# Memory keys and values in another order, 512-column value matmuls, column norms, and three moved steps

## The reference

```
mkv  = rmsnorm(mem_prompt, g_mem) @ w_mem_kv          # 256 memory tokens -> 4 heads x 256 keys, 4 heads x 256 values
xn   = rmsnorm(x, g_mix);  cq, ... = split_in(xn @ w_in)
branch_c = softmax(cq . mk / 16) @ mv                 # prompt tokens against these keys and values
branch_b = attention of 8 query heads over the chosen keys   # softmax over key rows, two heads at a time
h    = x + merged @ w_out
u    = rmsnorm(h, g_ffn) @ w_up                       # then convolution, gate, w_down, final rmsnorm
```

## Time and profile before

| | us |
|---|---|
| median of three runs (2171.22 to 2172.59) | 2171.45 |
| the profiled execution | 2170.77 |
| its span on the core | 2169.2 |
| TensorE busy | 2152.0 (99%) |
| VectorE busy | 1222.6 (56%) |
| ScalarE busy | 904.4 (42%) |
| GpSimd busy | 103.9 (5%) |

### The profile page before, as it was taken

One profiled execution on the slowest core, in us unless ns is written; L12 is line 12 of the kernel. 1 busy time (PEld: TensorE's weight loads), 2 busy tenths in 40 slices (PEclk: granted clock), 3 DMA queues, 4 the chain that ended last, 5 costly groups with the idle time before them and its releaser, 6 DMA issues.

```text
span 2169.2 us, 40311 instructions
## 1 busy us (share of the span) xinstructions
PE 2152.0 (99%) x14759; PEld 2126.8 (98%) x14759; DVE 1222.6 (56%) x1928; ACT 904.4 (42%) x1520; POOL 103.9 (5%) x152
## 2 busy tenths in 40 slices
PE   9999999999999999999999999999999999999998
PEld 9999999999999999999999999999999999999998
DVE  8745655444644444444445666656665566656675
ACT  6434433333443333333333444444444444444455
POOL 2202300001300000000000000000000000000000
PEclk9999999999999999999999999999999999999999
DMA  8644444444334444444454444454444543454443
GB/s 292 222 160 129 159 149 135 146 136 135 103 127 155 146 156 148 145 155 147 154 195 146 138 143 155 137 170 138 154 126 157 163 148 131 152 166 144 150 138 126
DMA packets 96625, 329.43 MB, mean 152 GB/s; under 512 B 11656, under 2 KB 19976, under 8 KB 96400
## 3 DMA queue, kind: packets, MB, share of 16 engines
q1 hardware_dynamic: 92928, 315.97, 45.0%
q0 software_dynamic: 3456, 9.49, 1.5%
q10 hardware_dynamic: 144, 2.62, 0.3%
HBM read 321.30 MB, written 6.73 MB: 151 GB/s over the span
## 4 chain that ended last, share of the span: by engine, by line
PE 95%; DVE 3%; DMA 1%; ACT 1%; issue 0%; SPq 0%; DVEq 0%; ACTq 0%
PE bank L542 29%; PE bank L543 29%; PE bank L544 29%; PE bank L581 3%; PE bank L578 1%; DVE w_lo L1317 1%; PE bank L873 1%; PE bank L875 1%; PE bank L874 1%; PE bank L572 0%; DMA hT<-in_xT 0%; PE bank L573 0%; PE bank L574 0%; PE bank L561 0%; PE bank L562 0%; PE bank L563 0%
## 5 line engine op out<-in xcount | busy, mean ns | idle before, releaser
L542 PE MATMUL bank<-xn_hi,w_hi 128*128 128x320 f32 (+1 forms) x3088 | 958.6, 310 | 3.3 <-DVE w_lo L1317 3.3
L544 PE MATMUL bank<-xn_hi,w_lo 128*128 128x320 f32 (+1 forms) x3088 | 953.2, 309 | 0.0
L543 PE MATMUL bank<-xn_lo,w_hi 128*128 128x320 f32 (+1 forms) x3088 | 953.2, 309 | 0.0
L1317 DVE TENSOR_TENSOR w_lo<-w_raw,w_hi 128x1024 fp32r<-128x1024 f32 x625 | 745.1, 1229 | 344.3 <-ACT w_hi L924 342.4
L924 ACT CAST w_hi<-w_raw 128x1024 fp32r<-128x1024 f32 x625 | 631.2, 1047 | 177.4 <-PE bank L544 155.0
L542 PEld LDWEIGHTS bank<-xn_hi,w_hi 128*128 128x128 f32 x3088 | 580.5, 188 | 8.1 <-issue 3.1
L543 PEld LDWEIGHTS bank<-xn_lo,w_hi 128*128 128x128 f32 x3088 | 580.6, 188 | 0.4
L544 PEld LDWEIGHTS bank<-xn_hi,w_lo 128*128 128x128 f32 x3088 | 580.6, 188 | 0.0
L543 PE MATMUL bank<-y_lo,w_hi 128*128 128x320 f32 x616 | 189.9, 308 | 0.0
L544 PE MATMUL bank<-y_hi,w_lo 128*128 128x320 f32 x616 | 189.9, 308 | 0.0
L542 PE MATMUL bank<-y_hi,w_hi 128*128 128x320 f32 x616 | 189.9, 308 | 0.0
(11 more groups left out here) (329 smaller groups left out, 2085.7 us busy)
## 6 DMA issues: line engine op xcount, KB each, us to landing
w_raw<-in_w_in SPq DMA_DIRECT2D x210, 512.0 KB, 3.8
w_raw<-in_w_up SPq DMA_DIRECT2D x176, 512.0 KB, 3.7
w_raw<-in_w_down SPq DMA_DIRECT2D x64, 512.0 KB, 3.5
w_raw<-in_w_branch SPq DMA_DIRECT2D x48, 512.0 KB, 3.4
...
```

The lines of the kernel that those rows point to most:

```text
L542: pe.matmul(out, h, hi[:, k0 + k, c0:n], start=un == 0 and k == 0, stop=False)
L543: pe.matmul(out, h, lo[:, k0 + k, c0:n], start=False, stop=False)
L544: last = pe.matmul(out, l, hi[:, k0 + k, c0:n], start=False, stop=un == len(units) - 1 and k == nk - 1)
L1317: dve.tensor_tensor(wlo[:, pl.slot(j), :, :], raw[:, pl.slot(j), :, :], f32(whi[:, pl.slot(j), :, :]), ALU.subtract).then_inc(w_lo, 1)
```

## The change

- **Order of the memory units.** For each quarter of the memory rows come k of head 0, half of v of heads 0 and 1, k of head 1, and the other half; then k of head 2, eight units of v of heads 2 and 3, and k of head 3. A v unit now has 256 rows x 512 columns: 12 matmuls of 512 columns. Each token half has one of the banks G, and each head's keys have a bank of their own.
- **Norms.** TensorE sums the squares into columns (one value per partition, for 128 tokens at a time), DVE computes the inverse root on 2 or 3 columns, multiplies them into a diagonal, and TensorE spreads the diagonal over all partitions (`inverse_rows`, before units 14 and 21). The sums stand before units 12 and 19.
- **Steps around it.** The loads and splits of the memory tokens come two units later or so (SP 3, 5, 7 for 1, 3, 5), v is read out after units 16 and 28 (two heads at once), k after units 15, 16, 20 and 31, x is scaled after units 21 to 29, and the scores of branch C wait for all keys.
- **First query softmax.** `q_exps(0)` stands at tile 3, behind the casts of that tile.
- **hT.** The first two of its 16 row blocks come in a transfer of their own ahead of the rest.
- **sum(h^2).** The matmul stands between the two units of the first feed-forward tile instead of behind both.

```diff
-KV_UNITS = [(kind, 0, n) for n in range(4) for kind in "kv"] + [(kind, h, n) for h in range(1, CHD) for kind in "kv"
-                                                              for n in range(4)]
-KV_LAST = {j: (kind, h) for j, (kind, h, n) in enumerate(KV_UNITS) if n == 3}
-U_CQ, T_CQ = len(KV_UNITS), 2 * CHD
-MEM_SUM, X_SUM = 7, 19
+KV_UNITS = [u for n in range(4) for u in (("k", 0, n), ("v", 0, 2 * n), ("k", 1, n), ("v", 0, 2 * n + 1))]
+KV_UNITS += [("k", 2, n) for n in range(4)] + [("v", 1, n) for n in range(8)] + [("k", 3, n) for n in range(4)]
+KV_LAST = {(kind, h): j for j, (kind, h, n) in enumerate(KV_UNITS)}
+U_CQ, T_CQ = len(KV_UNITS), CHD
+MEM_SUM, MEM_ROW, X_SUM, X_ROW = 12, 14, 19, 21
...
-        nvar = sums_at("norm_var", [3, T])
+        nvar = sums_at("norm_var", [3, 4])
+        diag = sums_at("inverse_diagonal", [T])
...
+        K_BANKS = (M[4], M[5], M[2], M[3])
...
-            after = {1: (lambda: mem_chunk(1),), 3: (lambda: mem_chunk(2), identity), 5: (lambda: mem_chunk(3),),
+            after = {3: (lambda: mem_chunk(1),), 5: (lambda: mem_chunk(2), identity), 7: (lambda: mem_chunk(3),),
...
-            def k_unit(pl, t, j, un):
+            def k_unit(pl, head, j, un):
...
-                        out, c = G[pl.bank(t)][:, e * NMEM:e * NMEM + NMEM], slice(e * P, e * P + P)
+                        out, c = K_BANKS[head][:, e * NMEM:e * NMEM + NMEM], slice(e * P, e * P + P)
...
-            def v_unit(pl, t, j, un):
-                h, l = v_units(whi, pl.slot(j)), v_units(wlo, pl.slot(j))
-                for k in range(4):
+            def v_unit(pl, j, un):
+                h, l = (w[:, pl.slot(j), :, :].rearrange("p (k four) c -> p k (four c)", four=4) for w in (whi, wlo))
+                for k in range(2):
                     for m in range(2):
-                        out, tok = G[pl.bank(t)][:, m * 256:m * 256 + 256], slice(m * P, m * P + P)
-                        k_ = 4 * un + k
-                        pe.matmul(out, mhi[:, k_, tok], h[:, k, :], start=k_ == 0 and m == 0, stop=False)
+                        out, tok = G[m][:, :], slice(m * P, m * P + P)
+                        k_ = 2 * un + k
+                        pe.matmul(out, mhi[:, k_, tok], h[:, k, :], start=k_ == 0, stop=False)
                         pe.matmul(out, mhi[:, k_, tok], l[:, k, :], start=False, stop=False)
-                        last = pe.matmul(out, mlo[:, k_, tok], h[:, k, :], start=False, stop=k_ == KT - 1 and m == 1)
+                        last = pe.matmul(out, mlo[:, k_, tok], h[:, k, :], start=False, stop=k_ == KT - 1)
...
-            def square_sums(n, width):
+            def square_sums(n, starts):
                 pe.wait_ge(ident_in, 16)
                 pe.wait_ge(x_sum if n else t_sum, 1)
-                total, ones = sq_sum[:, n, 0:width], K[:, C_ONE:C_ONE + P]
-                last = mm(M[n][:, 0:width], ones, total)
-                if n == 0:
-                    for m in range(2):
-                        last = mm(M[0][:, NMEM + m:NMEM + m + 1], sq_sum[:, 0, m * P:m * P + P], ones[:, 0:1])
+                for u, t in enumerate(starts):
+                    last = mm(M[n][:, u:u + 1], sq_sum[:, n, t:t + P], K[:, C_ONE:C_ONE + 1])
                 last.then_inc(t_tot, 1)
+            def inverse_rows(n, width):
+                pe.wait_ge(t_dg, n + 1)
+                mm(M[n][:, 0:width], K[:, C_ONE:C_ONE + P], diag[:, 0:width]).then_inc(t_row, 1)
...
-                pe.wait_ge(c_kf, h + 1)
+                pe.wait_ge(c_kf, CHD)
...
                 if j == MEM_SUM:
-                    square_sums(0, NMEM)
+                    square_sums(0, (0, P))
+                if j == MEM_ROW:
+                    inverse_rows(0, NMEM)
                 if j == X_SUM:
-                    square_sums(1, T)
-                t = 2 * h + (kind == "v")
-                if un == 0:
-                    pe.wait_ge(bank_read[plc.bank(t)], plc.bank_free(t))
+                    square_sums(1, (0, P, T - P))
+                if j == X_ROW:
+                    inverse_rows(1, T)
+                if kind == "v" and un == 0:
+                    for m in range(2):
+                        pe.wait_ge(bank_read[m], plc.bank_free(2 * h + m))
                 pe.wait_ge(*((w_lo, plc.through(j)) if j else (lo_first, 1)))
-                (k_unit if kind == "k" else v_unit)(plc, t, j, un)
+                if kind == "k":
+                    k_unit(plc, h, j, un)
+                else:
+                    v_unit(plc, j, un)
...
-            multiply(pl, 0, [(0, xhi, xlo, 0, UK), (1, xhi, xlo, UK, UK)], T, parts=(h_lo, KT))
-            pe.wait_ge(h_sum, KT + 1)
-            mm(M[0][:, 0:T], K[:, C_ONE:C_ONE + P], hacc[:, 0:T]).then_inc(sums, 1)
+            def h_sums():
+                pe.wait_ge(h_sum, KT + 1)
+                mm(M[0][:, 0:T], K[:, C_ONE:C_ONE + P], hacc[:, 0:T]).then_inc(sums, 1)
+            multiply(pl, 0, [(0, xhi, xlo, 0, UK), (1, xhi, xlo, UK, UK)], T, parts=(h_lo, KT), between=h_sums)
...
+            def v_tokens(p):
+                act.wait_ge(t_inv, 1)
+                act.wait_ge(w_used, pl.through(KV_LAST["v", p]))
+                for m in range(2):
+                    act.activation(mv[:, 2 * p:2 * p + 2, m, :], G[m][:, :].rearrange("p (h c) -> p h c", h=2), ACT.Identity,
+                                   scale=mnv[:, m:m + 1]).then_inc(bank_read[m], 1)
+                for m in range(2):
+                    act.wait_ge(bank_read[m], pl.bank_read(2 * p + m))
+                act.sem_inc(c_mvn, 2)
+            after = {0: (lambda: mem_squares(0),), 1: (lambda: mem_chunk(1),), 2: (lambda: mem_squares(1),),
+                     4: (lambda: mem_chunk(2),), 6: (lambda: mem_squares(2),), 8: (lambda: mem_chunk(3),),
+                     9: (lambda: mem_squares(3),), 12: (lambda: root(1, 2, nvar),), 16: (lambda: v_tokens(0),),
+                     19: (lambda: root(2, 3, nvar),)}
+            for c in range(4):
+                after[10 + 2 * c] = after.get(10 + 2 * c, ()) + (lambda c=c: x_squares(c),)
+            for q in range(8):
+                after[21 + q] = after.get(21 + q, ()) + (lambda q=q: x_hi(q),)
+            after[KV_LAST["v", 1] + 1] += (lambda: v_tokens(1),)
...
+                if t == 3:
+                    q_exps(0)
...
-                    q_exps(i - 1)
+                    if t > 2:
+                        q_exps(i - 1)
...
-            act.dma_start(hT[:, :, :].rearrange("p k t -> p (k t)"), a["xT"]).then_inc(hT_in, 16)
+            for k0, k1, done in ((0, 2, hT_in), (2, KT, hT_rest)):
+                act.dma_start(hT[:, k0:k1, :].rearrange("p k t -> p (k t)"), a["xT"][:, k0 * T:k1 * T]).then_inc(done, 16)
...
-            def mem_inverse():
-                dve.wait_ge(t_tot, 1)
-                rms(0, NMEM + 2, M[0][:, 0:NMEM + 2], nvar)
+            def inverse_columns(n, widths):
+                cols = len(widths)
+                dve.wait_ge(t_tot, n + 1)
+                rms(n, cols, M[n][:, 0:cols], nvar)
                 own.settle()
-                dve.tensor_copy(mnv[:, :], nvar[:, 2, NMEM:NMEM + 2])
-                dve.tensor_copy(minv[:, :], nvar[:, 2, 0:NMEM]).then_inc(t_inv, 1)
-                dve.wait_ge(t_inv, 1)
-                dve.wait_ge(c_raw, 1)
-                dve.tensor_tensor(kf[:, 0, 0, :], kf[:, 0, 0, :], minv[:, :], ALU.mult)
-                dve.tensor_tensor(kf[:, 0, 1, :], kf[:, 0, 1, :], minv[:, :], ALU.mult).then_inc(c_kf, 1)
-            def x_inverse():
-                dve.wait_ge(t_tot, 2)
-                rms(1, T, M[1][:, 0:T], nvar)
+                if n == 0:
+                    dve.tensor_copy(mnv[:, :], nvar[:, 2, 0:2]).then_inc(t_inv, 1)
+                    dve.wait_ge(ident_in, 16)
+                else:
+                    dve.wait_ge(t_row, 1)
+                t = 0
+                for u, width in enumerate(widths):
+                    last = dve.tensor_scalar(diag[:, t:t + width], ident[:, P - width:P], nvar[:, 2, u:u + 1], None, ALU.mult)
+                    t += width
+                last.then_inc(t_dg, 1)
+            def inverse_row(n, out, width):
+                dve.wait_ge(t_row, n + 1)
+                own.did(dve.tensor_copy(out[:, :], M[n][:, 0:width]))
                 own.settle()
-                dve.tensor_copy(inv[:, :], nvar[:, 2, 0:T]).then_inc(t_inv, 1)
-                dve.wait_ge(t_inv, 2)
+            def k_features(h):
+                dve.wait_ge(w_used, pl.through(KV_LAST["k", h]))
+                for e in range(2):
+                    last = dve.tensor_tensor(kf[:, h, e, :], K_BANKS[h][:, e * NMEM:e * NMEM + NMEM], minv[:, :], ALU.mult)
+                last.then_inc(c_kf, 1)
...
-            after = {0: (lambda: square_part(0),), 1: (lambda: mem_los(4), lambda: mem_los(5)),
-                     2: (lambda: square_part(1),), 3: (lambda: mem_los(6), lambda: mem_los(7)),
-                     4: (lambda: square_part(2),), 5: (lambda: square_part(3), square_sum),
```

(19 more changed lines are left out.)

52 lines of the change are left out of this document (11 added, 41 removed).

## The result

| | before | after |
|---|---|---|
| median of the runs | 2171.22 us (5 runs, 2169.32 to 2172.59) | 2159.34 us (5 runs, 2159.13 to 2159.65) |
| ratio | | 0.9949, 95% interval 0.9938 to 0.9960 |
| profiled execution, its span | 2170.77 us, 2169.2 us | 2159.49 us, 2157.7 us |

A forecast was written before the change was run, and what follows sets the result against it. TensorE's matmul stream, busy 99% of the span, was taken as the bound; 2.5 + 3.8 + 1.6 + 1.0 + 3.7 - 0.75 = 11.85 us from 2170.77 gave 2158.9, stated as 2159.2, range 2155.8 to 2164.0.

The forecast's parts named there:

- Width: v units of the memory stage: 512-column matmuls at 226 ns remove 192 matmuls and save 2.5 us, bounds 0 to 5.0.
- The rival by the 2.5 ns of the Trainium skill: v matmuls: only 2.5 ns saved for each of 192, 0.5 us, giving 2161.2; width without gain had chance 0.12.
- Memory holes: Memory stage: three TensorE idle times of 1.19, 1.10 and 0.76 us, each plus 0.26, go; 3.8 us saved.
- the holes of 73.31 and 77.21: TensorE idle 1.10 and 0.76 us in the memory stage, blamed on DVE's 5.5 us norm of x ahead of `w_lo`.
- the first hole: TensorE idle 1.19 us at 39.75, memory stage: ACT waited 3.95 us for DVE's inverse rms before reading the first v.
- Small matmuls: Memory stage: six new single-column passes for x and two more returns to the stream cost 0.75 us, between 0.3 and 1.2.
- Softmax: Query stage: casts ahead of the first softmax remove TensorE's 1.35 us idle time plus 0.26; 1.6 us saved.
- hT: Output projection: a small first transfer ends DVE's 5.75 us wait for 2.6 MB; 0.75 + 0.26 = 1.0 us saved.
- Sum of h squared: Feed-forward start: the sum one unit earlier closes the 1.91 us hole and slow-clock stretch, with 0.5 us to spare; 3.7 us saved.
- The diagonal: Before memory units 14 and 21 TensorE waits for DVE's diagonal of inverse norms; claimed ready in time by 1 to 2 us.
- holes that came back: Memory-stage rival: late diagonal, late loads or DVE out of lead return up to 3.8 us; 2160 to 2163, chance 0.10.

## Why the prediction was right

**Width: right, a little too large.** Forecast 226 ns per 512 columns and 2.5 us; measured 228.2 ns and, with all else equal, 2.32 us. The rest beside the columns grew from 13 to 15 ns. The rival by the 2.5 ns of the Trainium skill, "TensorE: Matmul & The Clock Gate", section "Back-to-back issue gap" (an estimate of 512 / 2.4 + 2.5 = 215.8 ns per matmul), is refuted by this kernel's steps. The section gives that formula for a matmul by itself, which the prediction didn't say.

**Memory holes: right in size, half wrong in reason.** All three went. The 3.8 us were not measured for all three together; for the holes of 73.31 and 77.21, forecast at 2.4, the kernel with columns at the old place shows 94.87 - 92.89 + 0.41 = 2.4 us. But the step that gave these two holes to the narrow operations named one of two sufficient causes. The place alone does it, and the columns of x cost 0.41 us that the kernel needn't pay. Of the two cures the prediction counted on the dearer one. The reason given for the first hole, ACT's early read of v, was not undone by itself.

**Small matmuls: too large.** +0.75 was taken, within 0.3 to 1.2; the columns of x cost 0.41, and if the three holes gave the 3.83 us that were forecast, the stretch leaves 89.10 - (94.87 - 2.32 - 3.83) = 0.38 for all of them.

**The start was left out.** From unit 0 to unit 1 the profile after takes 0.91 us longer: unit 0 begins 0.29 us sooner, and unit 1 0.62 us later, since its weights land at 9.68 us instead of 9.07. That is more than the 0.4 us saved on the small matmuls. In the other profiles of kernels with the new load order that stretch takes between 3.0 and 4.7 us, so much of the 0.91 belongs to this one execution. Unit 1 began at 11.56 to 12.38 us in the twelve profiles with the new load order and at 11.54 and 10.88 in the two with the old: a small loss by the order of the loads is possible, and was not tried.

**Softmax, hT: right**, 1.60 and 0.87 to 1.01 for 1.6 and 1.0.

**Sum of h squared: right for the profiled execution.** 3.7 forecast, 3.71 measured, with a margin of 0.6 us where 0.5 was forecast. The step took the slow clock for a sure consequence of the hole; it followed in some executions only. 2.2 us are gained in every profile, 1.5 more where the clock would have fallen.

**The diagonal: the margin was forecast right without the reason for its size.** 1 to 2 us were forecast; most profiles that leave the norm and the order as the change made them have 1.5 to 1.7, the one after the change 0.3. GpSimd's share (two splits and the diagonals 3 us longer) was in no term of the sum.

**The range** of 2155.8 to 2164.0 was wide: its lower end needed a width without any fixed part, its upper end holes that came back. Neither happened. That the median comes within 0.2 us of 2159.2 is in part luck: the loss at the start and the small matmuls taken too large nearly cancel, and 2159.2 was chosen between the two values that the profiled execution and the median of the kernel before led to, 2158.9 and 2159.6.
